# One inference step of a hybrid decoder in float32: the order of the attention steps on four engines, a projection chunk in step 6 of each pair, sample values in two halves

## What is computed

```python
def stick_breaking(q, k, v, bias, q_pos, k_pos):
    z = einsum('bthd,bshd->bhts', q, k) * (HEAD_DIM ** -0.5) + bias
    causal = k_pos[None, :] < q_pos[:, None]
    log_beta = log_sigmoid(z)
    log_rest = where(causal, log_sigmoid(-z), 0.0)
    after = cumsum(log_rest, axis=3, reverse=True) - log_rest
    a = where(causal, exp(log_beta + after), 0.0)
    return einsum('bhts,bshd->bthd', a, v)
```

## Time and profile before

| | |
|---|---|
| median of 3 runs | 2921.88 us |
| the profiled execution | 2921.54 us, its span 2919.5 us |
| PE busy | 2763.1 us, 95% of the span |
| DVE, ACT, POOL busy | 46%, 26%, 41% |
| attention, pairs 0 to 7 | from 1186.5 us (first scores) to 2020.1 us |
| granted PE clock, mean | 0.955 of full speed |

### The profile page before, as it was taken

The page is one execution under the profiler, slowest core; times in us unless marked ns, Lnnn a source line. Parts: engine busy times, 40 slices in busy tenths (PEclk is TensorE's granted clock), DMA queues, the critical chain, the costliest instruction groups (busy, mean ns, idle before and its releaser), DMA issues.

```text
span 2919.5 us, 41661 instructions
## 1 busy us (share of the span) xinstructions
PE 2763.1 (95%) x16657; PEld 2637.8 (90%) x16657; DVE 1350.9 (46%) x1237; ACT 755.1 (26%) x1080; POOL 1205.0 (41%) x542
## 2 busy tenths in 40 slices
PE   7999999999999999899999999967999999999997
PEld 6989999999999999788787878756999999999997
DVE  5244543333333337566766766663543333333335
ACT  5122210000000002456665655653110000000003
POOL 4542454334433343344444444443454333433340
PEclk9999999999999999899988989966999999999999
DMA  3111111111111112221221122121121111111111
GB/s 111 51 31 37 44 58 45 51 44 44 44 51 44 44 44 94 61 61 39 64 60 36 53 66 63 32 91 67 43 59 44 46 50 44 44 44 51 44 37 60
DMA packets 219619, 152.91 MB, mean 52 GB/s; under 512 B 9258, under 2 KB 207714, under 8 KB 219426
## 3 DMA queue, kind: packets, MB, share of 16 engines
q1 hardware_dynamic: 200930, 139.63, 15.9%
q10 hardware_dynamic: 18496, 10.49, 1.2%
HBM read 128.86 MB, written 21.22 MB: 51 GB/s over the span
## 4 chain that ended last, share of the span: by engine, by line
PE 83%; DVE 6%; issue 5%; POOL 3%; ACT 2%; DMA 0%; ACTq 0%; SPq 0%; POOLq 0%; DVEq 0%
PE ps L706 48%; PE ps L835 17%; PE aux L963 6%; PE ps L889 2%; PE ps L916 2%; DVE sp_part L1572 2%; PE ps L871 2%; PE ps L901 2%; POOL a_part L644 1%; DVE scratch L1423 1%; PE aux L935 1%; PE aux L1005 1%; DVE sp_part L1570 1%; DVE sp L1559 1%; POOL w_raw L634 1%
## 5 line engine op out<-in xcount | busy, mean ns | idle before, releaser
L564 POOL TENSOR_TENSOR w_hi<-w_raw,ones_col 128x1024 fp32r<-128x1024 f32 x146 | 281.1, 1925 | 997.6 <-PE ps L706 674.2
L571 POOL TENSOR_TENSOR w_lo<-w_raw,w_hi 128x1024 fp32r<-128x1024 f32 x167 | 467.6, 2800 | 13.1
L644 POOL TENSOR_TENSOR a_part<-zb,a_part 128x256 fp32r<-128x256 f32 (+2 forms) x96 | 200.9, 2093 | 466.3 <-ACT zb L1243 466.3
L706 PE MATMUL ps<-near_hi,w_hi 128*128 128x352 f32 x1632 | 356.9, 327 | 17.0 <-DVE near_lo L1410 13.1
L706 PE MATMUL ps<-near_lo,w_hi 128*128 128x352 f32 x1632 | 354.2, 325 | 0.0
L706 PE MATMUL ps<-near_hi,w_lo 128*128 128x352 f32 x1632 | 352.8, 324 | 0.0
L706 PEld LDWEIGHTS ps<-near_hi,w_hi 128*128 128x128 f32 x1632 | 278.8, 190 | 21.1 <-issue 11.5
L706 PE MATMUL ps<-in_hi,w_hi 128*128 128x352 f32 x1320 | 286.6, 325 | 4.8 <-issue 3.9
L1537 DVE TENSOR_TENSOR h<-h,ps 128x1056 f32<-128x1056 f32 x160 | 200.2, 1251 | 187.3 <-PE ps L835 187.3
L706 PE MATMUL ps<-in_lo,w_hi 128*128 128x352 f32 x1320 | 285.3, 324 | 0.0
L706 PE MATMUL ps<-in_hi,w_lo 128*128 128x352 f32 x1320 | 283.9, 323 | 0.0
(11 more groups left out here) (218 smaller groups left out, 4501.2 us busy)
## 6 DMA issues: line engine op xcount, KB each, us to landing
w_raw<-in_w_gate_dram SPq DMA_DIRECT2D x44, 512.0 KB, 3.8
w_raw<-in_w_up_dram SPq DMA_DIRECT2D x44, 512.0 KB, 3.8
w_raw<-in_w_down_dram SPq DMA_DIRECT2D x44, 512.0 KB, 3.6
w_raw<-in_a_w_in_dram SPq DMA_DIRECT2D x16, 512.0 KB, 3.9
k_page<-in_cache_k_dram SPq DMA_DIRECT2D x128, 64.0 KB, 1.9
v_page<-in_cache_v_dram SPq DMA_DIRECT2D x128, 64.0 KB, 1.9
h_kept<-h SPq DMA_DIRECT2D x8, 528.0 KB, 2.7
h<-h_kept SPq DMA_DIRECT2D x8, 528.0 KB, 7.3
```

The source lines that it names most:

```text
L564: gp.tensor_tensor(hi, raw, one, ALU.mult).then_inc(w_hi_done, 1)
L571: gp.tensor_tensor(lo, raw, as32(hi), ALU.subtract).then_inc(w_ready, 1)
L644: gp.tensor_tensor(a_part[:, 1, :, c0:TB], zb[:, s % 3, :, c0:TB], as32(a_part[:, 0, :, c0:TB]), ALU.subtract).then_inc(a_split, 1)
L706: last = mm(out[:, c, 0:CH], w[:, ks], x[:, k, c * CH:c * CH + CH], start=(k == 0 and n == 0), stop=(k == KT - 1 and n == 2))
```

## The change

- On PE a step becomes: scores of s, the chunk, the triangle of s-1, turned rows, sample work, **values of s-2, remainder of s-1**. So values and remainder come ahead of the next scores instead of behind them.
- On ACT `weights` of s-2 comes ahead of `biased` of s instead of behind it. On DVE `softplus` and `softplus_split` of s-1 come first, then `capped` of s, then `k_low`, `chunk_evicted` and `logits` of s-1. DVE's `out` (the finished output of a half, which waits for ACT's copy `crossed`) comes ahead of `k_low` and `chunk_evicted`.
- Step 6 gets chunk 5, and the chunks behind it move one step forward; step 9 now has none. POOL's last slab of weights moves with them.
- The sample values are issued as 8 products at the end of step 10 and 8 in step 11.
- The last pair needs one step less to drain. The mask `s_mask` is made on POOL ahead of the first attention weights' splits instead of behind them.

```diff
@@ -118,16 +118,17 @@
 CP = (384, 384, 256)
 
 
-X1 = {0: ("c", 0), 1: ("p", 1), 2: ("c", 1), 3: ("c", 2), 4: ("c", 3), 5: ("c", 4), 6: ("p", 3), 7: ("c", 5),
-      8: ("c", 6), 9: ("c", 7), 10: ("c", 8)}
-X2 = {0: ("p", 0), 2: ("k", 0), 3: ("k", 1), 4: ("k", 2), 5: ("p", 2), 9: ("v", 0), 10: ("v", 1), 11: ("v", 2)}
+X1 = {0: ("c", 0), 1: ("p", 1), 2: ("c", 1), 3: ("c", 2), 4: ("c", 3), 5: ("c", 4), 6: ("c", 5), 7: ("c", 6),
+      8: ("c", 7), 10: ("c", 8)}
+X2 = {0: ("p", 0), 2: ("k", 0), 3: ("k", 1), 4: ("k", 2), 5: ("p", 2), 6: ("p", 3), 8: ("v", 0), 9: ("v", 1),
+      11: ("v", 2)}
 X_ORDER = [x[s] for s in range(NS) for x in (X1, X2) if s in x]
 AUX_ORDER = [item for item in X_ORDER if item[0] != "c"]
 NA = len(AUX_ORDER)
 CHUNK_STEP = {s: item[1] for s, item in X1.items() if item[0] == "c"}
 
 S_START, S_SCORES = 0, {1: (0,), 2: (1,), 6: (2,), 7: (3,)}
-S_CAP, S_LOG, S_SOFT, S_LATER, S_EXP, S_VALUES = 8, 8, 9, 9, 10, 11
+S_CAP, S_LOG, S_SOFT, S_LATER, S_EXP, S_VALUES = 8, 8, 9, 9, 10, (10, 11)
 V_SPLIT, OUT1, OUT0 = 2, 10, 2
 O_AT = 4
 
@@ -601,15 +602,7 @@
                     split(q0 + n, 0, 0, n % 2, None, 0, 4)
 
             ffn_splits(0)
-            for n in range(2):
-                scaled += 1
-                split(Q_KQV + n, 0, 0, n, (G_KV, G_MIX1)[n], scaled, 4 if n == 0 else 2)
-            for n in range(2, 5):
-                scaled += 1
-                split(Q_KQV + n, 0, 0, n % 2, (G_KV, G_MIX1, G_KV)[n % 3], scaled, 4 if n == 2 else 2)
-
-            pool.wait_ge(tile_done, T_KQV)
-            pool.wait_ge(sq_added, 4 * KT)
+            pool.wait_ge(sq_added, 3 * KT)
             gp.memset(s_mask[:], 0.0).then_inc(s_mask_done, 1)
             pool.wait_ge(s_mask_done, 1)
             gp.affine_select(out=s_mask[:], in_=s_mask[:], pattern=[[DL, DB], [0, 2], [1, DL]], compare_op=ALU.is_gt,
@@ -617,6 +610,13 @@
             pool.wait_ge(s_mask_done, 2)
             gp.affine_select(out=s_mask[:], in_=s_mask[:], pattern=[[-DL, DB], [0, 2], [0, DL]], compare_op=ALU.is_ge,
                              fill=MASKED, base=0, channel_multiplier=1).then_inc(s_mask_done, 1)
+            for n in range(2):
+                scaled += 1
+                split(Q_KQV + n, 0, 0, n, (G_KV, G_MIX1)[n], scaled, 4 if n == 0 else 2)
+            for n in range(2, 5):
+                scaled += 1
+                split(Q_KQV + n, 0, 0, n % 2, (G_KV, G_MIX1, G_KV)[n % 3], scaled, 4 if n == 2 else 2)
+
             def split_part(part, i, at, gain, n_scaled, used):
 
                 q, half, par = at + 6 * i, at // 2 + 3 * i, at % 2
@@ -660,8 +660,8 @@
                         split_part(s + 1, i, q + 1, G_MIX1 if more else None, scaled + 3 * p, 9 * p)
                     if more and s in (4, 5, 6):
                         split_part(s - 4, i, q + 2, G_KV, scaled + 3 * p + 1, 9 * p + 3)
-                    if more and s in (8, 9, 10):
-                        split_part(s - 8, i, q + 3, None if last_slabs else G_KV, scaled + 3 * p + 2, 9 * p + 6)
+                    if more and s in (7, 8, 9):
+                        split_part(s - 7, i, q + 3, None if last_slabs else G_KV, scaled + 3 * p + 2, 9 * p + 6)
                     if more and s == 11:
                         split_part(0, i, q + 4, None if last_slabs else G_MIX1, scaled + 3 * p + 3, 9 * p + 9)
                     if not more and s - O_AT in range(PAIRS - 1):
@@ -995,35 +995,39 @@
                     mm(zs[0:RS, 2 * SC:3 * SC], neg_tri[0:RS, 0:RS], s_sp[0:RS, 2, :], start=False, stop=True,
                        skip_group_check=True).then_inc(s_c, 1)
 
-            def sample_values(p, c):
-                pe.wait_ge(s_ad, p + 1)
-                pe.wait_ge(vp_in, 16 * DB * PAGES * (p + 1))
-                mm(os_, v_row[0:RS, RT, :], s_a[0:RS, 2, :], start=True, stop=False, skip_group_check=True)
-                for n in range(DB * PAGES):
+            def sample_values(p, c, half):
+                if half == 0:
+                    pe.wait_ge(s_ad, p + 1)
+                    pe.wait_ge(vp_in, 16 * DB * PAGES * (p + 1))
+                    mm(os_, v_row[0:RS, RT, :], s_a[0:RS, 2, :], start=True, stop=False, skip_group_check=True)
+                for n in range(half * DB, half * DB + DB):
                     b, j = divmod(n, PAGES)
                     at = b * 2 * DL
                     last = mm(os_[:, at:at + 2 * DL], v_page[:, n, :], s_a[:, j, at:at + 2 * DL],
                               start=False, stop=(n == DB * PAGES - 1), skip_group_check=True)
-                last.then_inc(s_pv, 1)
+                if half == 1:
+                    last.then_inc(s_pv, 1)
 
             def pair(p, c, more=True):
-                for s in range(NS + (0 if more else 3)):
+                for s in range(NS + (0 if more else 2)):
                     if s < NS:
                         scores(p, c, s)
-                    for lag, work in ((3, values), (2, carry)):
-                        at = lagging(p, c, s, lag)
-                        if at is not None:
-                            work(*at)
                     if s in X1 and (more or X1[s][0] == "p"):
                         x_turn(p, c, X1[s], more)
-                    if s == S_VALUES:
-                        sample_values(p, c)
+                    if s == S_VALUES[1]:
+                        sample_values(p, c, 1)
                     at = lagging(p, c, s, 1)
                     if at is not None:
                         take_later(*at)
                     if s in X2 and (more or X2[s][0] == "p"):
                         x_turn(p, c, X2[s], more)
                     sample(p, c, s)
+                    if s == S_VALUES[0]:
+                        sample_values(p, c, 0)
+                    for lag, work in ((2, values), (1, carry)):
+                        at = lagging(p, c, s, lag)
+                        if at is not None:
+                            work(*at)
 
             def rows_of_first(x, src, ready):
                 pe.wait_ge(tile_out, ready)
@@ -1320,11 +1324,13 @@
 
             def pair(p, c, more=True):
                 act.wait_ge(bias_done, p + 1)
-                for s in range(NS + (0 if more else 3)):
-                    for lag, work in ((0, biased), (2, weights), (0, exp_part)):
+                for s in range(NS + (0 if more else 2)):
+                    for lag, work in ((2, weights), (0, biased), (0, exp_part)):
                         at = lagging(p, c, s, lag) if lag or s < NS else None
                         if at is not None:
                             work(*at)
+                        if s == V_SPLIT and work == weights:
+                            v_high(p)
                     if more and s - 1 in CHUNK_STEP and CHUNK_STEP[s - 1] < 6:
                         k_high(p, c, CHUNK_STEP[s - 1])
                     if not more and s - O_AT in range(PAIRS - 1):
@@ -1342,8 +1348,6 @@
                     if s == S_EXP:
                         act.wait_ge(s_c, p + 1)
                         fn(s_a[:].rearrange("p j n -> p (j n)"), zs, ACT.Exp).then_inc(s_ad, 1)
-                    if s == V_SPLIT:
-                        v_high(p)
                     if s == OUT1:
                         crossed(p, 1)
                     if s == OUT0 and (not isinstance(p, int) or p > 0):
@@ -1636,11 +1640,19 @@
                         .then_inc(q_blk_done, 1)
                 vec.tensor_scalar(s_bias[:], head_bias[0:1, ds(2 * p, 2)].unsqueeze(1).unsqueeze(3)
                                   .to_broadcast([1, DB, 2, DL]), -1.0, None, ALU.mult).then_inc(q_blk_done, 1)
-                for s in range(NS + (0 if more else 2)):
-                    for lag, work in ((2, logits), (1, softplus)):
-                        at = lagging(p, c, s, lag)
-                        if at is not None:
-                            work(*at)
+                for s in range(NS + (0 if more else 1)):
+                    at = lagging(p, c, s, 1)
+                    if at is not None:
+                        softplus(*at)
+                        softplus_split(*at)
+                    if s == V_SPLIT:
+                        v_low(p)
+                    if s < NS:
+                        capped(p, c, s)
+                    if s == OUT0 and (not isinstance(p, int) or p > 0):
+                        out(p - 1, 0)
+                    if s == OUT1:
+                        out(p, 1)
                     if s == S_CAP:
                         dve.wait_ge(s_scored, 4 * p + 4)
                         vec.tensor_scalar(s_fn[:].rearrange("p j n -> p (j n)"), zs, SP_CAP, None, ALU.min)\
@@ -1651,20 +1663,11 @@
                                           s_fn[:].rearrange("p j n -> p (j n)"), ALU.max).then_inc(s_spd, 1)
                     if more and s - 2 in CHUNK_STEP and CHUNK_STEP[s - 2] < 6:
                         k_low(p, c, CHUNK_STEP[s - 2])
-                    if s < NS:
-                        capped(p, c, s)
```

(13 more changed lines are left out.)

## The result

The changed kernel takes 3009.76 us (3007.73 to 3021.7, 4 runs) against 2921.18 us (2920.06 to 2928.34, 4 runs): ratio 1.0306, 95% interval 1.0275 to 1.0338. It is slower, by 88 us where 51 were forecast. That lies inside the range of 2880 to 3015, but 10 us above the forecast's own 2945 to 3000. Its profiled execution answers to the earlier trace rows with this: the span; the row of line 981; windows with length, busy PE, PEld (PE's loads of weights), DVE, ACT, POOL, clock, DMA share and GB/s, one over the seven periods of line 981 and one over a single pair. That pair is the longest of the seven (108.0 to 118.9), since a turn of PE's loop over pairs is in it.

A forecast was written before the change was run, and what follows sets the result against it. PE sets the pace, busy 93.0 of 101.0 us a pair. With work 85, waits 20.5 and clock 5, a pair takes 110.5; six pairs +57, pair 0 nothing, last pair -6: 2921.5 + 51 = 2972, range 2880 to 3015.

The forecast's parts named there:

- the walk through a full step: DVE in a full step: `capped` held by `a_low`, `k_low` by POOL's part; eviction at 7.7 or 8.7, PE waits 1.7.
- Rival A: `k_low` goes ahead of POOL's part, eviction ends at 6.0 when PE wants it; 97.5 a pair, 2880 us; chance 0.24.
- Rival C: Nothing: half the forecast waits come, 10 us instead of 20 a pair, and eat the 10.3 gain; 2921 us; chance 0.07.
- Rival B: Waits of 1.6 us also lower PE's clock, chunks behind them start slow; 7 more a pair, 3015 to 3030; chance 0.09.
- The waits: PE's idle time in each pair, summed over its steps: 20.5 us, against 8.0 before.
- The clock: Lower PE clock behind three waits of 3.5 us or more: 5 us a pair in all, between 3 and 10.
- the two low stretches: PE at low clock behind step 6's wait, 3.2 us lost, and behind the sample values, about 2.8; both should go.
- The sum: Whole kernel: pairs 1 to 6 +57, pair 0 with the start 0, last pair -6; together +51, so 2972 us.
- The last pair and what follows: Last pair, without chunks: shorter cycle and one step less to drain, `capped` still held; -6 us, between -20 and +5.
- The most that the change could gain: Per pair: step 6's wait 4.3, its clock loss 3.2, and 2.8 from halved sample values; 10.3 us.
- the samples' softplus behind `capped`: Step 9, without a chunk: PE waits for the sample softplus, which stands behind `capped` on DVE; 3.5 us a pair.
- the 2.8 lost behind the sample values: PE's 5 us of work behind the sample values loses about 2.8 us to low clock; halves should save it.

The follow-up runs named there:

- both ways of taking the pairing out: Two separate edits of the changed kernel: DVE's `k_low` moved behind logits, 2942.43 us; POOL's weight parts made on 8 of 128 columns, 2939.55 us.
- mask, tables and halves: Kernel before plus early mask, moved chunks, turned rows and POOL parts, and sample values in halves; PE, ACT and DVE lists not reordered: 2894.1 us.
- both DVE placements mended: Changed kernel with `k_low` behind logits and the samples' two steps ahead of `capped` on DVE, chunk eviction still behind `capped`: 2920.41 us.
- k_low last: Changed kernel with one move on DVE, `k_low` behind logits and so behind the chunk's eviction: 2942.43 us, ratio 1.0068.

## Why the prediction was right in kind, and off in size

**The mechanism** was right and is shown: the walk through a full step with POOL's part between `capped` and `k_low` is in the rows, and both ways of taking the pairing out give back 67 and 70 us. What the prediction understated is that `k_low` was often held before, too: 1020 ns on average, not the 0.55 of the earlier trace rows. No run shows what that cost there; `capped` stood behind it, and not the eviction. Rival A hung on `k_low` going ahead of POOL's part; in the rows above it goes behind, as in the earlier trace rows. The prediction cites a rule (the Trainium skill, SBUF — State Buffer, Who interferes with whom: the one that starts first keeps the shared pair of ports for the whole instruction). The traces agree: `k_low` took 2.71 us instead of 0.55 and ended 0.42 behind POOL's part. On what the rule leaves open, who goes when both wait, the one that had asked first went here too. Rival C fell with the size. Rival B's condition did not come: behind the waits of 1.5 (step 5) and 1.7 us (step 8) the clock stayed full, 1.00 from 1431.0 to 1463.5 and from 1469.6 to 1492.2. Its kind of cost was real, from other waits, as shown next.

**The waits**, step by step in the pair from 1407.8, forecast and measured: step 0: 1.9 and 0; step 1: 2.0 and 2.1; step 2: 3.8 and 0.9 (3.9 in the pair before); step 4: 1.6 and 0.9; step 5: 1.6 and 1.5; step 6: 3.6 and 2.7; step 8: 1.6 and 1.7; step 9: 3.5 and 3.3. Over the seven periods PE was idle for 14.7 a pair, where the forecast had 20.5: too much by 5.8, although the turns of the loop (0.8 a pair) were not in it. Steps 0 and 2 are most of it.

**The clock** is the term that failed: "5 in all, between 3 and 10". At 0.87 it costs 798.8 x 0.13 / 7 = 14.8 a pair. I had let it cost 5, less than the 8.1 that I had read for the kernel before, on the ground that the two low stretches go and each new one hides partly in the next wait. The same pair, divided at its low stretches, shows why not (behind each stretch its length; the number behind POOL's is the clock):

```profile
1407.80:1420.60 12.80, 10.68 (x56) 8.96 (x56) 7.92 (x11) 8.13 (x15) 5.99 (x4) 0.74 0.29 79
...
1425.10:1431.00 5.90, 5.87 (x35) 5.00 (x36) 3.33 (x5) 2.90 (x5) 1.93 (x1) 0.71 0.39 125
1431.00:1463.50 32.50, 27.29 (x158) 22.59 (x156) 27.78 (x25) 20.21 (x28) 15.46 (x6) 1.00 0.06 20
1463.50:1469.60 6.10, 6.03 (x27) 4.43 (x28) 3.38 (x5) 2.76 (x4) 0.70 (x1) 0.72 0.44 129
...
1492.20:1499.30 7.10, 7.00 (x27) 5.55 (x28) 3.31 (x5) 2.70 (x7) 2.89 (x2) 0.52 0.00 0
...
1504.80:1523.10 18.30, 15.55 (x69) 13.90 (x69) 11.24 (x16) 7.49 (x14) 6.43 (x4) 0.53 0.23 65
```

Length times missing clock gives 3.3 behind the wait of 2.1 in step 1, 1.7 behind the 0.9 of step 2, 1.7 behind the 2.7 of step 6, 3.4 behind the 3.3 of step 9, and 8.6 from just ahead of the second half of the sample values to the chunk behind the turn of the loop. The forecast had three stretches, each half hidden. It had none for step 1, none for the turn, and took the one at the sample values as gone. Between them, through the waits of 0.9 and 1.5 in steps 4 and 5, the clock is full. PE's work without waits and clock, 99.4 - 14.8 = 84.6, is the 85 of the forecast. (The 14.8 is an estimate, as the mean clock takes in idle stretches; by the same sum the kernel before has 9.1 at its 0.91, and the 5.7 between them is close to the 5.9 by which PE's busy time grew.) So a pair is 84.6 + 14.7 + 14.8 = 114.1, where the forecast had 85 + 20.5 + 5 = 110.5: two errors, of -5.8 and +9.8, partly cancel.

**The sum**: pairs 1 to 6 had +57. The periods of line 981 in pairs 0 to 6 took +91.7 against a forecast of 57 + 7 = 64; this is the larger part of the miss. The start gave -7.0, as forecast. The last pair and what follows: +3.9 against -6. Its waits for the split fell from 30.8 to 24.4 us, but 5.0 came for the samples and for `out`. No run isolates this stretch. With the old lists it took 1017.0, 1013.2 (mask alone) and 1020.2 (mask, tables and halves), so a difference of 3.9 is not clear of their spread.

**What it hides.** The most that the change could gain, 10.3 a pair, was overrated: 3.0 came from the tables and nothing from the halves. And the samples' softplus behind `capped`, which the prediction priced at 3.5 in step 9, was as large a wait as it said, 3.2 a pair (22.4 over seven). Taking it out gave 22 us, but mostly as clock. One sum of the prediction is off by a little: the 2.8 lost behind the sample values would be 3.4 by its own proportion, 3.2 of 4.7 on 5 us.

**Left open.** The 26 us between the changed kernel with both DVE placements mended (2920) and the old lists with mask, tables and halves (2894). PE's waits there are for `a_low` (16.2), turned rows (9.0) and the turns of the loop (5.8), in the stretch from 1290 to 1870; no run took the first two out. Here PE's own new order and lag, the rival of the experiments, may still have its share: no run has the new lists on DVE and ACT with PE's old one, or the other way round.

## What to carry to other kernels

When an engine that shares a resource with another gets a new list, write out the chain at the place where both want it, and put what a third engine waits for (here an eviction that the other does not hold) ahead of what the other can hold, but never ahead of an instruction whose input is ready while its own is not. Price a wait twice, for itself and for the clock behind it: of the 13.1 us a pair lost here 5.9 were clock. Test each part of a change by itself: in this one two tables were worth 23 us, and the reordered lists that came with them cost 115 (3009.8 against 2894.1).

## What the runs showed of the hardware

In the pair divided above PE's clock returned inside a chunk at the end of each of the five low stretches. At a turn of the loop in the kernel with k_low last, in PE's timeline, matmuls of one form fall from 0.52 to 0.34 us some 5.8 us after the work resumes:

```profile
1490.46 0.98 PE L901 MATMUL ps<-sp_part,neg_rest_r 128*128 128x384 f32 x4 [0.25 <-DVE zb L1582]
1494.49 0.90 PE L871 MATMUL ps<-kq 64*128 64x128 f32 x6 [3.06 <-issue]
...
1499.47 0.52 PE L963 MATMUL aux<-in_hi,w_hi 128*128 128x384 f32 x1
...
1500.32 0.34 PE L963 MATMUL aux<-in_hi,w_hi 128*128 128x384 f32 x1
```

A turn of PE's loop shows up as idle time, the more so the later a wait stands ahead of it. In the changed kernel logits ends at 1513.60 and the scores behind the turn start at 1518.13, 4.5 us later (4.7 at the other turn, 4.1 in the kernel with k_low last); in the kernel before it was 4.4 from the end of the split's low part, the last thing that PE waited for (1479.07), to the scores (1483.46). What differs is how much work PE has left between: 1.78 us or 3.19, so the idle time is 2.75 or 1.20. The loop has three passes, and two turns show such a wait, 5.7 us together. Written out, both waits are gone and the run is 12 us shorter. But the two periods with a turn shrink by only 1.7 and 1.5 us; three others take 4.5, 6.2 and 3.3 less, and two take 4.9 and 1.1 more. So the 12 us are measured, and that they are the price of the turns is not shown; the trace does not say what PE does in the idle time either.
